# Value chunks stored 64 bytes further on in two widened weight slots, with three small moves in the two attentions

## What is computed

```
h = x
mix = hgrn2_mixer(h, ...)            # layer 1: q,f,i,g = h @ w_in; "values" are i = h @ w_in[:, 2048:3072]
h = layer_norm(ALPHA*h + mix);  h = layer_norm(ALPHA*h + conv_ffn(h))
k, v = split(h @ shared_w_kv)
mix = swa_sink_mixer(h, k, v, ...)   # layer 2: 16 heads, window of 128, softmax with a sink
h = layer_norm(ALPHA*h + mix);  h = layer_norm(ALPHA*h + conv_ffn(h))
# third layer on rms_norm(h): pooling, "fox" attention with forget gates (8 heads), memory attention (4 heads)
logits_mem = q_m . k_m * scale                       # 256 memory tokens
logits_fox = q_b . k_b * scale + F[t] - F[s], F = cumsum(log_sigmoid(f_b + b_f))
x = h + concat(y_pool*silu(g_a), y_fox*silu(g_b), y_mem*silu(g_m)) @ w_out
```

## Time and profile before

| | |
|---|---|
| median of 3 runs | 1490.79 us (1489.32 to 1492.55) |
| profiled execution | 1492.55 us, of which the span from first to last instruction is 1490.7 |
| TensorE, matmuls | busy 1460.6 us, 98% of the span, 9390 instructions |
| VectorE / ScalarE / GpSimd | busy 859.9 (58%) / 616.0 (41%) / 482.0 us (32%) |
| mean granted TensorE clock | 0.997 |

### The profile page before, as it was taken

The page is one execution under the profiler, slowest core; times in us unless marked ns, Lnnn a source line. Parts: engine busy times, 40 slices in busy tenths (PEclk is TensorE's granted clock), DMA queues, the critical chain, the costliest instruction groups (busy, mean ns, idle before and its releaser), DMA issues.

```text
span 1490.7 us, 23774 instructions
## 1 busy us (share of the span) xinstructions
PE 1460.6 (98%) x9390; PEld 1214.8 (81%) x9390; DVE 859.9 (58%) x1261; ACT 616.0 (41%) x780; POOL 482.0 (32%) x360
## 2 busy tenths in 40 slices
PE   8999999999999999999999999999999999999999
PEld 6787887998888888899777988888888897777777
DVE  7787686676665560165685666656630274565741
ACT  5565554353223231245664442232221355654541
POOL 0000000224545554432221145445454514422222
PEclk9999999999999999999999999999999999999999
DMA  7422123403232223323112122222323312312211
GB/s 220 135 75 87 58 86 106 150 29 113 84 107 90 98 99 115 119 76 114 57 40 75 57 86 85 90 107 86 111 85 113 127 58 85 132 70 71 71 53 61
DMA packets 23600, 137.24 MB, mean 92 GB/s; under 512 B 2600, under 2 KB 5208, under 8 KB 8672
## 3 DMA queue, kind: packets, MB, share of 16 engines
q1 hardware_dynamic: 18288, 124.79, 23.7%
q10 hardware_dynamic: 5232, 11.32, 2.8%
HBM read 131.89 MB, written 4.21 MB: 91 GB/s over the span
## 4 chain that ended last, share of the span: by engine, by line
issue 41%; PE 27%; POOL 24%; DVE 3%; DMA 2%; ACT 1%; DVEq 1%; ACTq 0%; POOLq 0%; SPq 0%
POOL WL L454 15%; POOL WL L463 9%; PE pair L489 7%; PE pair L490 7%; PE pair L491 7%; DMA RAW<-stream 1%; PE pair L1086 1%; PE pair L674 1%; PE pair L1073 1%; DVE WL L1661 1%; ACT WH L1192 1%; PE pair L1005 1%; PE pair L1063 1%; PE pair L703 1%; DMA H<-x_t 0%
## 5 line engine op out<-in xcount | busy, mean ns | idle before, releaser
L489 PE MATMUL pair<-AH,WH 128*128 128x512 f32 (+1 forms) x1240 | 474.2, 382 | 9.2 <-DVE AL L1650 6.6
L454 POOL TENSOR_TENSOR WL<-RAW,WH 128x512 fp32r<-128x512 f32 x228 | 309.9, 1392 | 480.4 <-ACT WH L1192 480.4
L490 PE MATMUL pair<-AL,WH 128*128 128x512 f32 (+1 forms) x1240 | 463.3, 374 | 0.0
L491 PE MATMUL pair<-AH,WL 128*128 128x512 f32 (+1 forms) x1240 | 463.2, 374 | 0.0
L1192 ACT ACTIVATE WH<-RAW 128x2048 fp32r<-128x2048 f32 x106 | 202.9, 1914 | 456.8 <-PE pair L491 447.7
L463 POOL TENSOR_TENSOR WL<-RAW,WH 128x512 fp32r<-128x512 f32 x128 | 172.0, 1376 | 510.2 <-ACT WH L1192 510.2
L489 PEld LDWEIGHTS pair<-AH,WH 128*128 128x128 f32 x1240 | 234.0, 189 | 58.1 <-issue 16.2
L491 PEld LDWEIGHTS pair<-AH,WL 128*128 128x128 f32 x1240 | 234.0, 189 | 41.8
L490 PEld LDWEIGHTS pair<-AL,WH 128*128 128x128 f32 x1240 | 234.2, 189 | 40.8 <-issue 1.9
L2030 DVE TENSOR_SCALAR CA<-pair,PAR 128x512 f32<-128x512 f32 x88 | 67.2, 805 | 148.8 <-PE pair L491 145.8
L489 PE MATMUL pair<-GH,WH 128*128 (+2 forms) x416 | 149.1, 358 | 0.0
(11 more groups left out here) (249 smaller groups left out, 1895.8 us busy)
## 6 DMA issues: line engine op xcount, KB each, us to landing
RAW<-stream SPq DMA_DIRECT2D x114, 1024.0 KB, 4.9
H<-x_t SPq DMA_DIRECT2D x5, 512.0 KB, 8.1
bias_rows<-ROWS ACTq DMA_DIRECT2D x1, 2048.0 KB, 24.3
BIAS<-bias_rows ACTq DMA_DIRECT2D x1, 2048.0 KB, 7.7
FBC<-forget_rows ACTq DMA_DIRECT2D x4, 512.0 KB, 3.8
out<-H ACTq DMA_DIRECT2D x8, 256.0 KB, 2.0
H<-x_t SPq DMA_DIRECT2D x1, 1024.0 KB, 10.5
RAW<-stream SPq DMA_DIRECT2D x3, 256.0 KB, 7.3
```

The source lines that it names most:

```text
L454: pool.tensor_tensor(WL[w][:, part], RAW[raw][:, part], WH[w][:, part].bitcast(F32), ALU.subtract).then_inc(w_lo, 1)
L489: pe.matmul(out_, wh, xh, start=start, stop=False, skip_group_check=shared)
L490: pe.matmul(out_, wh, xl, start=False, stop=False, skip_group_check=shared)
L491: return pe.matmul(out_, wl, xh, start=False, stop=stop, skip_group_check=shared)
```

## The change

Four edits. (1) The four value chunks are rounded and split to a place 16 floats (64 bytes) into their slots, and read from there; to make room, WH of slots 0 and 1 and WL of slot 0 grow by 32 floats and WL of slot 1 by 16; the unused 192 bytes go. (2) In the window attention the m=1 part of units 3, 4, 7 and 8 stands directly behind the m=0 part, ahead of `sw_turn`. (3) `score(0)` waits for a new semaphore `z_taken`, which VectorE gives with line 2149, in place of `z_abs`. (4) `split_next(N_GM)` moves from the end of u = 1 to u = 2, behind expo(3).

```diff
+NUDGE = 16
-        WH = [sb(f"WH{s}", [P, 2048], F32R) for s in range(2)]
-        WL = [sb(f"WL{s}", [P, 2048], F32R) for s in range(2)]
+        WHX = [sb(f"WH{s}", [P, 2048 + 2 * NUDGE], F32R) for s in range(2)]
+        WLX = [sb(f"WL{s}", [P, 2048 + (2 - s) * NUDGE], F32R) for s in range(2)]
+        WH, WL = ([w[:, 0:2048] for w in ws] for ws in (WHX, WLX))
+        WHN, WLN = ([w[:, NUDGE:2048 + NUDGE] for w in ws] for ws in (WHX, WLX))
...
-        sb("ROWS_SHIFT", [P, 48])
...
+        def weights_at(n, slot):
+            if isinstance(n, int) and n in HG_V:
+                return WHN[slot], WLN[slot]
+            return WH[slot], WL[slot]
+        def wcols(slot, n=None):
+            wh, wl = weights_at(n, slot)
...
-                wh, wl = wcols(slot)
+                wh, wl = wcols(slot, n)                # tok_chunk
...
-                if u in (3, 4, 7, 8):
-                    sw_half(2 + u // 6, (u - 1) % 4 - 1, 0)
-                if u in (5, 9):
-                    sw_half(2 + u // 6, 3, 0)
-                    sw_half(2 + u // 6, 3, 1)
+                if u in (3, 4, 5, 7, 8, 9):
+                    sw_half(2 + u // 6, (u - 2) % 4, 0)
+                    sw_half(2 + u // 6, (u - 2) % 4, 1)
...
-                if u in (3, 4, 7, 8):                  # behind sw_weigh(u - 1)
-                    sw_half(2 + u // 6, (u - 1) % 4 - 1, 1)
...
-            pe.wait_ge(z_abs, 1)
+            pe.wait_ge(z_taken, 1)
...
-                    act.activation(WH[w][:, :], RAW[raw][:, :], ACT.Copy).then_inc(w_hi, 1)
+                    act.activation(weights_at(n, w)[0][:, :], RAW[raw][:, :], ACT.Copy).then_inc(w_hi, 1)
...
                 if u + 1 < 20:
                     expo(u + 1)
+                if u == 2:
+                    split_next(N_GM)
...
-                    split_next(N_GM)                   # end of u == 1
...
-                    raw, wh, wl = RAW[n % 2][:, :], WH[n % 2][:, :], WL[n % 2][:, :]
+                    wh, wl = weights_at(n, n % 2)
+                    raw, wh, wl = RAW[n % 2][:, :], wh[:, :], wl[:, :]
...
-            dve.tensor_scalar(FG_[:, 0], bk(1)[0:8], par["forget_b"][0:8], None, ALU.add)
+            dve.tensor_scalar(FG_[:, 0], bk(1)[0:8], par["forget_b"][0:8], None, ALU.add).then_inc(z_taken, 1)
```

More of the change, by code:

```diff
@@ L282, in build @@
         sg_made, pool_w_loaded, sink_put = sem("sg_made"), sem("pool_w_loaded"), sem("sink_put")
-        z_abs, z_exp, f_made, f_stored = (sem(n) for n in ("z_abs", "z_exp", "f_made", "f_stored"))
+        z_taken, z_abs, z_exp, f_made, f_stored = (sem(n) for n in ("z_taken", "z_abs", "z_exp", "f_made", "f_stored"))
         f_bcast = [sem("f_bcast0"), sem("f_bcast1")]
@@ L286, in build @@
         out_ready, stored = sem("out_ready"), sem("stored")
-        def wcols(slot):
-            return (WH[slot][:, :].rearrange("p (k c) -> p k c", k=8), WL[slot][:, :].rearrange("p (k c) -> p k c", k=8))
+        def weights_at(n, slot):
[4 more added lines that the diff above has]
+            wh, wl = weights_at(n, slot)
+            return (wh[:, :].rearrange("p (k c) -> p k c", k=8), wl[:, :].rearrange("p (k c) -> p k c", k=8))
         def wrows(slot):
```

## The result

| | time, us | profiled execution: span, us |
|---|---|---|
| before | 1490.05 median of 6 (1488.75 to 1494.19) | 1490.7 |
| after | 1497.06 median of 6 (1496.42 to 1498.07) | 1494.6 |

Ratio 1.0042, 95% interval 1.0032 to 1.0052: the change made the kernel 7.0 us slower, where 1.7 us faster was forecast. The time lies 5.5 us above the forecast range.

The account below looks back on a forecast made before the run. TensorE, busy 98% of the span, was taken as the bound. Edits 1 to 4 summed to 0 + 0.4 + 0.2 + 1.1 = 1.7 us off the median 1490.79, giving 1489.1 us, range 1486.4 to 1491.6.

Parts of the forecast that it names:

- I take zero for these as well: Edit 1: tensors behind the slots move (parameters and constants 448 bytes, working area 256); cost taken as zero.
- if TensorE's matmuls of other chunks change pace: Sign that the prediction is wrong: TensorE's matmuls outside the value chunks run at another pace.
- 13 ns a matmul: Value chunks: fixed part of 0.120 us over 0.107; as a loss on 384 matmuls it costs 5.0 us, giving 1494.1.
- 64 bytes leave the read pattern what it was: Edit 1, value chunks: 64 bytes are four whole 16-byte lines, so the read pattern stays; effect taken as zero.
- VectorE's equal subtractions: Edit 1 evidence: VectorE's 34 subtractions, of both slots and all chunk kinds, lie between 1205 and 1246 ns.
- the new address speeds them: Rival, value chunks: half to all of 0.013 us a matmul goes, 2.5 to 5 us, about 1485; chance 0.07.
- slows: Rival: the new address slows value chunks, a loss from 4.4 ns a matmul; 13 ns gives 1494.1; chance 0.06.
- 0.4 was taken, of at most 0.76: Edit 2, window attention: units 3, 4, 7, 8 give 0.19 us each, 0.76 together; 0.4 taken as arriving.
- The wait ahead of it stays: Window attention: argument against the half-clock stretch changing, that the wait ahead of that stretch remains.
- the rival that had 0.09: Window attention: the half-clock stretch disappears, worth 1.7 us, giving 1487.4; chance 0.09.
- none of the edits depends on which run it is: The sum: reason for taking the 1.7 us gain from the median 1490.79, not the slower profiled run.
- the forecast sum is 1.3: Last attention: edit 3 gains 0.2 us at the scores, edit 4 gains 1.1 at unit 3's transposes.

Follow-up runs that it names:

- e1_moves: The kernel before with edits 2, 3 and 4 on the old layout: 1487.70 us against 1490.05, ratio 0.9981.
- q_act128: The kernel before with AH, AL and all four weight halves moved on by 128 bytes, the OH/OL stream left in place: 1499.05 us against 1490.38 (1 run).
- e3_aligned: The changed kernel, all four edits, with both weight slots at the old place modulo 256 bytes, value chunks 64 bytes off: 1486.86 us, ratio 0.9977.
- p_64_192: The kernel before with slot 0 placed 64 bytes and slot 1 192 bytes off the activations modulo 256: 1505.13 us against 1490.05 (1 run).

## Why the prediction was wrong

- **Edit 1, the layout: the step that failed.** "I take zero for these as well" was said of what stands behind the slots, and for the slots themselves I asked only whether the 384 value matmuls would change pace. Slot 1's start moved too, and with it the weights of every second chunk. The prediction's own sign of being wrong, "if TensorE's matmuls of other chunks change pace", came true. It costs (11.157 - 10.88) / 48 = 5.8 ns a matmul. With the matmuls of both profiled executions numbered in order of their start, the kernel after lies behind e1_moves by 0 us at matmul 3000 (275.4 and 275.5), by 3.8 at 5000 (671.77, 667.93), by 8.1 at 8000 (1215.5, 1207.4) and by 9.7 at the last (1491.05, 1481.38). The first feed-forward's share is 4.0, and its 14 slot-1 chunks by 0.28 make 3.9. In the records of before some 3460 matmuls behind number 3000 follow at the 512-column pace (225 to 228 ns apart); with about half of them in slot 1, 1730 x 5.8 ns = 10.0 us, where the records have 9.7. Ahead of it are some 440, worth 1.3 us by the same sum, and the value chunks give back 1.4: nothing is left there, as the records say. By the medians it is 9.4.
- **Why the profile did not show it.** The trace of before has one relative place for all weights and streams, so its even pace (10.88 in both slots) was evidence of nothing about addresses. I said that of the value chunks, and let them gain or, in a rival, lose 13 ns a matmul. The same 13 ns on the matmuls of a moved slot would have given over 20 us either way (1730 x 13 ns). That 64 bytes leave the read pattern what it was did not hold either: places that all differ by multiples of 32 bytes have different paces, in both kinds of matmul. VectorE's equal subtractions told of a writer, which indeed did not change, and nothing of TensorE's reading.
- **Value chunks.** The rival "the new address speeds them" was right in kind: 11.31 for 11.50, and in the kernel after 5.74 + 5.84 for 5.84 + 6.15 in each of the later three, 1.4 us in all, where it expected 2.5 to 5. The rival "slows", held at 0.06, named the right mechanism (an address changes TensorE's pace, deciding from a few ns a matmul) for the wrong matmuls.
- **Edit 2.** Units 7 and 8 gained 0.24 and 0.23 us, where 0.19 was worked out, and 0.6 us arrived where 0.4 was taken, of at most 0.76. "The wait ahead of it stays" did not hold fully: 1.9 us became 1.4. The half-clock stretch is not in the kernel after, the rival that had 0.09; it was priced at 1.7 us (by its own terms, a quarter of 6.42, 1.6) and cost 2.5 in the profiled execution of before. So "none of the edits depends on which run it is" was unsafe: that execution was one at 0.997, and if edit 2 is what removes the stretch its gain depends on the execution.
- **Edits 3 and 4.** The waits went and came as forecast (0.69 for 0.7 at `score(1)`, none at unit 3). The records have 1.24 us for the two, the forecast sum is 1.3.
- **The sum.** Without edit 1 the forecast was a gain of 1.7 us. The records give 0.62 + 1.24 = 1.9, and the totals 2.35 (1.5 to 4.2 by the interval), with what the half-clock stretch adds. So the mechanism of edits 2 to 4 was right, and their sizes nearly. The one term costed at zero without a row that bore on it was larger than all others and of the other sign.

The Trainium skill, "TensorE: Matmul & The Clock Gate", Part 2 (Step-by-step: what each phase is for), gives TensorE "two independent SBUF read ports", one for the stream and one for the weight loads, and says that loading the next weights takes no read bandwidth from the running matmul. The Trainium skill, "SBUF — State Buffer", Who interferes with whom, says that PE and ACT never wait on anyone. Neither section speaks of start addresses, and the runs show that the pace is not independent of them: with the same instructions, a chunk takes 10.88 or 11.20 us by where the weights start against the stream (q_act128). Whether the ports, the memory behind them or something else causes it, no run here shows.

## What to carry to other kernels

Before a tensor changes size, work out where everything behind it goes, modulo 256 bytes, and keep the operands that TensorE loads and streams at their old distance; then the gain of a change can be seen. Where the trace has only one address for an operand, its steady pace bounds nothing: multiply a few ns by every matmul that reads the moved tensors, not only by those that the change is about. In e3_aligned another order of the slots, in as much memory, turned 7.0 us slower into 3.2 us faster (2.4 at 0.999 or above).

## What the hardware showed that was not expected

- The pace of 48 float32r matmuls of 512 columns, weights and stream both split floats, depends on the distance of their starts: 10.88 us at 0 modulo 256 bytes, 10.99 to 11.24 at seven other places of the first feed-forward. The distance doesn't settle it alone: at 192 bytes the second feed-forward of p_64_192 has 11.00 and 11.20 in turn. At 128 bytes it was 11.157 with slot 1 alone displaced, 11.20 with both slots, and 11.21 with the high half of slot 1 alone.
- In value chunks (tokens loaded, 256 columns of weights streamed) 0 is not the best: 11.51, 11.20, 11.31 and 11.52 us for 96 matmuls at 0, 32, 64 and 128 bytes. At 64 bytes there are two paces: the second halves of the later chunks took 5.84 us in the kernel after, against 6.06 in e3_aligned and p_64_192, and in p_64_192 the first half of chunk 6 took 5.53, against 5.74 in chunk 10. Medians from start to start are 113 ns in the fast halves and 118 in the others; what chooses is open.
- The rounding (1914 ns) and the subtraction (1396 ns) didn't change with these addresses.
